# Half of the gate chunks moved into the last attention unit and the sample attention, which runs in four 32-column tiles

## The chip, the cores and the metric

The kernel runs on one core of one Trainium2 chip. The metric is the device time in microseconds of one execution. TensorE (PE in the profile) multiplies, VectorE (DVE), ScalarE (ACT) and GpSimd (POOL) work element by element, SyncE (SP) mostly issues transfers (DMA).

## What is computed

One layer of a decoder trunk, for a prompt of 1024 tokens and 8 sample sequences of 8 new tokens (T = 1088 tokens in all), D = 1024. The parts that matter here, from the reference:

```python
h = rmsnorm(x, p['pre_mix_norm'])
u = h @ p['w_in']                      # q,k,v of 3 groups, z, xbc, dt, gate_raw (2*D_MODEL columns)
# branch A: dilated attention; groups (128,1), (512,4), (2048,16), 8 heads of 64
# branch B: Mamba-2 SSD, 4 groups of 8 heads, chunked scan, gated group norm
a_proj = a_out @ p['w_attn_out']
b_proj = y @ p['w_ssd_out']
gate_a = jax.nn.sigmoid(gate_raw[..., :D_MODEL])
gate_b = jax.nn.sigmoid(gate_raw[..., D_MODEL:])
mixed = (gate_a * a_proj + gate_b * b_proj) @ p['w_out']
x = x + rmsnorm(mixed, p['post_mix_norm'])
# then a SwiGLU feed-forward with w_up and w_down

# sample attention, one sequence b with its 8 queries:
g = jnp.take(kv_all, jnp.maximum(idx, 0).reshape(-1), axis=1)     # idx = past_rows + i - j*dil
s = jnp.einsum('bshe,bskhe->bshk', q, g[:, :, :, 0]) * ATTN_SCALE
p, lse = masked_softmax_stats(s, valid)
o = jnp.einsum('bshk,bskhe->bshe', p, g[:, :, :, 1])
```

In the sample attention the softmaxes of the three groups are merged by their denominators, which is one softmax over all keys of the three groups. The 1024 past positions give 128 + 512 + 512 loaded rows per batch (of the third group 8 rows of every 16), and each batch has 24 new rows.

## The kernel before

**Layout and precision.** Activations lie transposed, channels on the partitions, tokens in three parts TH = 0:384, 384:736, 736:1088 (part c uses PSUM bank G[c]; the other five banks are A[0..4]). Each f32 operand of the big products is split into a high and a low fp32r half (hH, hL; wH, wL), and a product takes three matmuls per k-step (L2173 to L2175): hi x hi, lo x hi, hi x lo. A weight chunk is 1024 x 128 columns (512 KB): SP loads it into one of two raw buffers (wraw), GpSimd splits it (L775, L777) into one of three slots (wH, wL), TensorE uses it for the three parts. The order of chunks and of the uses of a bank is fixed by numbers: C_SSD, C_ATT, C_PROJ, C_OUT, C_FF count chunks (semaphore w_split), U_SSD, U_ATT, U_SAM, U_PROJ count uses of a bank (g_ready when filled, g_free when emptied).

**Stages, in order.** (1) norm and transposes; (2) the state-space stage, a loop over 4 groups (`group`): conv chunks, z chunks between the steps of the scan, then a state loop of four passes hp, then the output product of the group with w_ssd_out; (3) attention of the prompt, 12 units (j, gr), j = 0..3 pairs of heads, gr = 0..2 groups, each of 8 token tiles, with the q, k, v products of the next unit between the tiles (`qkv_part`); the last unit (3,2) has no next one; (4) sample attention, 8 batches b; (5) projection, gating (`mix`) and output product; (6) feed-forward.

**The state loop.** In pass hp TensorE transposes the s0 state of two heads (L2368, 8 transposes of 128x128) and VectorE and ScalarE copy the result out (s0t; ScalarE at L1173, behind its four Silus of zs, L1146). Then two parts of gate chunk hp (`tile(10 + hp, ..., only=c)`), the cm matmuls (L2379, 32 columns each, on two column tiles), the bm matmuls (L2383), and the third part of the gate chunk. So 4 gate chunks (GT = 4) belong to each group, 16 in all. ScalarE makes the sigmoid and stores it to gate_scr (`gate_part`). s0 has two buffers: a pass's state is stored, then the state of the pass after the next is loaded into the same buffer.

**Sample attention.** Per batch SP loads the keys (kraw, 9 tiles of 128 rows x 512) when those of the batch before are transposed, and the values (vraw) when the batch's value product is done. `scores(b + 1)` runs ahead of `values(b)`. TensorE transposes five key tiles per pair of heads (L2532), ScalarE copies them (L1295), and a 64-column product gives the scores of groups 0 and 1 (L2545, L2548). The keys of group 2 are multiplied and reduced on VectorE (`own_keys`) against the query rows, replicated through q_scr in DRAM; the values of group 2 are weighed and added on VectorE too (`weigh`). The scores against the new rows are computed in unit (3,2) (`new_scores`) and go through n_scr in DRAM; `new_rows` writes the new k and v rows to the outputs there, one group after the other. The softmax: masked minima on VectorE (L1876), exponential on ScalarE (L1299), scaling on VectorE (L1885). The value product is one of 64 columns with 512 moving columns per tile (L2589). Between batches 1 and 2 the prompt's attention output (atok) is transposed on four banks (L2612) and split into aH (L1323) and aL (L1940). GpSimd builds the block-diagonal queries (qblk).

**The gates.** The gates are loaded back from gate_scr and accm from ba_scr in the course of the sample attention, on SP.

## Time and profile before

| | us |
|---|---|
| median of 3 runs | 2932.91 |
| lowest, highest | 2931.29, 2938.15 |
| the profiled execution's own time | 2932.58 |
| its span | 2930.9 |

| engine | busy us | share of the span |
|---|---|---|
| PE (matmuls) | 2808.0 | 96% |
| PEld (weight loads) | 2624.9 | 90% |
| DVE | 1392.7 | 48% |
| ACT | 826.3 | 28% |
| POOL | 835.8 | 29% |

Times in the profile are microseconds from the start of the span. Matmuls overlap in the records, so the cost of one in a stream is the distance between starts, not its duration. An f32 matmul (not a transpose) stands as two records, an fp32r one as one. `x8` means eight records merged in one line. `[0.76 <-ACT ...]` is idle time of the engine before the line and what ended it. "128*32" is the stationary operand, rows x columns. The clock column is the granted TensorE clock, 1.00 for 2.4 GHz and 0.5 for 1.2 GHz, averaged over the stretch.

### The profile page before, as it was taken

The page shows a single profiled execution, that of the slowest core. Times are in us where ns is not written, and L with a number is a line of the kernel's source. Part 1 is how long each engine was busy: PE and PEld are TensorE (multiplying, and loading weights), DVE is VectorE, ACT ScalarE, POOL GpSimd, SP SyncE. Part 2 cuts the span into 40 slices and gives each one's busy share as a digit, 9 for nine tenths or more (in the row PEclk, how much of TensorE's full clock was granted, in tenths as well). Part 3 has the DMA queues.
Part 4 walks back from the last instruction along what each step waited for, and adds up shares of the span by engine and source line. Part 5 has one row for each costly group of instructions (what it writes and reads, how often), then busy time and mean ns, then how long its engine had stood idle before and what let it go on. Part 6 is the DMA issues. An engine that isn't in the chain of part 4 may idle for free.

```text
span 2930.9 us, 46443 instructions
## 1 busy us (share of the span) xinstructions
PE 2808.0 (96%) x17725; PEld 2624.9 (90%) x17725; DVE 1392.7 (48%) x2390; ACT 826.3 (28%) x1977; POOL 835.8 (29%) x554
## 2 busy tenths in 40 slices
PE   7999999999999999999999976889999999999997
PEld 5989998999999899999999963359999999999997
DVE  5485557647565762212323236677733333333334
ACT  4463155126414511333332332213410000000004
POOL 2342334324422434112121100024042323232332
PEclk9999999999999999999999988989999999999999
DMA  5545335344534532122231356973011111111111
GB/s 176 174 123 159 105 118 172 103 144 121 175 93 129 164 111 97 32 73 61 60 81 45 82 159 186 292 235 119 23 51 44 49 39 51 37 51 37 51 48 66
DMA packets 334137, 303.04 MB, mean 103 GB/s; under 512 B 26320, under 2 KB 302336, under 8 KB 332328
## 3 DMA queue, kind: packets, MB, share of 16 engines
q1 hardware_dynamic: 249464, 243.09, 27.1%
q10 hardware_dynamic: 84456, 56.93, 6.5%
q8 instruction: 152, 2.49, 0.3%
q14 instruction: 65, 0.53, 0.1%
HBM read 250.81 MB, written 102.91 MB: 121 GB/s over the span
## 4 chain that ended last, share of the span: by engine, by line
PE 89%; DVE 3%; DMA 3%; issue 2%; ACT 1%; POOL 1%; SPq 0%; ACTq 0%; DVEq 0%; POOLq 0%
PE ps L2173 24%; PE ps L2174 24%; PE ps L2175 24%; PE ps L2464 2%; PE ps L2443 2%; PE ps L2334 1%; PE ps L2330 1%; PE ps L2455 1%; PE ps L2548 1%; PE ps L2333 1%; PE ps L2532 1%; PE ps L2589 1%; DMA wraw<-in_w_out_dram 1%; DMA smqrep<-q_scr 1%; PE ps L2383 1%
## 5 line engine op out<-in xcount | busy, mean ns | idle before, releaser
L2173 PE MATMUL ps<-hH,wH 128*128 128x352 f32 (+1 forms) x2208 | 739.0, 335 | 8.7 <-issue 4.5
L2175 PE MATMUL ps<-hH,wL 128*128 128x352 f32 (+1 forms) x2208 | 722.4, 327 | 0.0
L2174 PE MATMUL ps<-hL,wH 128*128 128x352 f32 (+1 forms) x2208 | 722.2, 327 | 0.0
L775 POOL CAST wH<-wraw 128x1024 fp32r<-128x1024 f32 (+1 forms) x178 | 195.8, 1100 | 1550.3 <-PE ps L2175 1230.5
L777 POOL TENSOR_TENSOR wL<-wraw,wH 128x1024 fp32r<-128x1024 f32 (+1 forms) x178 | 443.6, 2492 | 14.3
L2173 PEld LDWEIGHTS ps<-hH,wH 128*128 128x128 f32 x2208 | 416.7, 189 | 33.8 <-issue 26.5
L2174 PEld LDWEIGHTS ps<-hL,wH 128*128 128x128 f32 x2208 | 417.2, 189 | 0.4
L2175 PEld LDWEIGHTS ps<-hH,wL 128*128 128x128 f32 x2208 | 416.1, 188 | 0.0
L2173 PE MATMUL ps<-mH,wH 128*128 128x384 f32 (+1 forms) x1128 | 371.4, 329 | 2.7 <-issue 2.7
L2174 PE MATMUL ps<-mL,wH 128*128 128x384 f32 (+1 forms) x1128 | 371.1, 329 | 1.0 <-issue 0.8
L2175 PE MATMUL ps<-mH,wL 128*128 128x384 f32 (+1 forms) x1128 | 370.1, 328 | 0.0
L1832 DVE COPY atp<-ps 128x256 f32<-128x256 f32 (+1 forms) x96 | 52.5, 547 | 363.1 <-PE ps L2455 363.1
L2173 PEld LDWEIGHTS ps<-mH,wH 128*128 128x128 f32 x1128 | 211.8, 188 | 4.3 <-issue 3.8
L2174 PEld LDWEIGHTS ps<-mL,wH 128*128 128x128 f32 x1128 | 211.6, 188 | 2.4 <-issue 1.9
L2175 PEld LDWEIGHTS ps<-mH,wL 128*128 128x128 f32 x1128 | 211.7, 188 | 0.0
L2173 PE MATMUL ps<-uH,wH 128*128 128x352 f32 (+1 forms) x528 | 174.3, 330 | 0.0
L2174 PE MATMUL ps<-uL,wH 128*128 128x352 f32 (+1 forms) x528 | 172.8, 327 | 0.0
L2175 PE MATMUL ps<-uH,wL 128*128 128x352 f32 (+1 forms) x528 | 172.8, 327 | 0.0
L2107 DVE TENSOR_TENSOR m<-m,ps 128x352 f32<-128x352 f32 (+1 forms) x240 | 123.4, 529 | 78.6 <-PE ps L2175 78.3
L1434 ACT ACTIVATE sq<-sq 128x352 f32<-128x352 f32 (+1 forms) x63 | 31.8, 507 | 416.3 <-DVE sq L2042 416.3
L949 ACT COPY qkv<-ps 128x384 f32<-128x384 f32 (+2 forms) x108 | 59.2, 548 | 311.4 <-PE ps L2175 273.0
L2088 DVE TENSOR_TENSOR sq<-sq,ps 128x352 f32<-128x352 f32 (+1 forms) x66 | 35.0, 532 | 220.0 <-PE ps L2175 220.0
(405 smaller groups left out, 4664.2 us busy)
## 6 DMA issues: line engine op xcount, KB each, us to landing
wraw<-in_w_in_dram SPq DMA_DIRECT2D x92, 512.0 KB, 3.9
wraw<-in_w_up_dram SPq DMA_DIRECT2D x44, 512.0 KB, 3.7
ssdcr<-cum_scr ACTq DMA_DIRECT2D x32, 512.0 KB, 4.5
out_dram<-in_cache_kv_w_dram SPq DMA_DIRECT2D x16, 960.0 KB, 5.5
smkraw<-in_cache_kv_w_dram SPq DMA_DIRECT2D x45, 256.0 KB, 7.1
wraw<-in_w_down_dram SPq DMA_DIRECT2D x22, 512.0 KB, 3.6
smkraw<-in_cache_kv_w_dram SPq DMA_DIRECT2D x9, 1024.0 KB, 6.4
smvraw<-in_cache_kv_w_dram SPq DMA_DIRECT2D x35, 256.0 KB
```

What stands on the lines that cost most here:

```text
L775: pool.tensor_copy(hi, a).then_inc(w_hi, 1)
L777: pool.tensor_tensor(lo, a, hi.bitcast(F32), ALU.subtract).then_inc(w_split, 1)
L949: ins = act.copy(dst, src)
L1434: act.activation(cols(sq[i], c), cols(sq[i], c), ACT.Silu).then_inc(gate_silu, 1)
L1832: dve.tensor_copy(pt[(i - 1) % 2][:, :, :].rearrange("p a b -> p (a b)")[:, 0:w], A[3][:, 0:w]).then_inc(pt_out, 1)
L2088: dve.tensor_tensor(cols(sq[i], c), cols(sq[i], c), gff(c, 2 * i + 2), ALU.mult).then_inc(g_free[c], 1)
L2107: dve.tensor_tensor(cols(m2[:, m, :], c), cols(m2[:, m, :], c), gff(c, m + 1), ALU.add).then_inc(g_free[c], 1)
L2173: pe.matmul(dst, hi, cols(mH[:, k, :], c), start=k == 0, stop=False)
L2174: pe.matmul(dst, hi, cols(mL[:, k, :], c), start=False, stop=False)
L2175: last = pe.matmul(dst, lo, cols(mH[:, k, :], c), start=False, stop=k == kt - 1)
L2443: mm = pe.matmul(score_half(gr, t, s), tokens(qT, gr, t)[rows], keys(kT, gr, t)[rows], start=True, stop=True)
L2464: mm = pe.matmul(A[4][:, 64 * s:64 * s + 64], pt[i % 2][:, s * len(bl) + b, :], vtok[gr][:, t, 64 * s:64 * s + 64], start=b == 0, stop=b = ...
```

## The change

Two gate chunks instead of four stay in each state-space group (GT = 2); a pass of the state loop now has three halves of a part (`gate_half`) at three places. Eight chunks move: three into unit (3,2), as its products (`unit_gate`), five into the sample attention, as 119 + 1 single k-steps at six places of each batch (`fill`, FILL). Their raw values are stored by ScalarE (`moved_store`), and the sigmoid is made after they are loaded back (`sigmoids`, in the projection stage, for rows 4 to 7 of each gate). The w_ssd_out chunks are six instead of four.

In the sample attention all three groups go through TensorE: 36 key transposes per batch on three banks, copied in turn by ScalarE and VectorE into buffers for the whole batch; the scores and the values as sets of four 32-column tiles (`quarter`), one per pair of heads, so that 128 partitions hold the scores; the new rows' scores are computed in each batch; the probabilities are not scaled, the output is. `own_keys`, `weigh`, q_scr, n_scr and newS go. The new k and v rows are transposed within units (3,1) and (3,2) (`sets`). The batches no longer overlap, and the loops over them are unrolled. The transposes of atok move into the last batch, on two banks. The buffers lie elsewhere (kraw and vraw over the qkv region), and so the loads of gates and accm come later on SP.

The diff, cut to what the prediction speaks of:

```diff
-GT = 4
+GT = 2
...
-U_SAM = U_ATT + NJ * NG * 3
+NGC = 2 * KD - GT * SG
+U_SAM = U_ATT + NJ * NG * 3 + 3
...
+WSSD = ((0, 2), (2, 2), (4, 1), (5, 1), (6, 1), (7, 1))
...
+        FILL = {(b, s): n for b in range(DB - 1) for s, n in enumerate((2, 2, 9, 1, 1, 2))}
+        FILL[DB - 1, 0] = 1
+        assert sum(FILL.values()) == (NGC - 3) * 3 * KD
...
-            firsts += [GATE0 + k * D + g * 2 * P + m * P for m in range(2) for k in range(2)]
+            firsts += [GATE0 + k * D + g * P for k in range(GT)]
             return [(win[:, :, ds(f, P)], KD, P) for f in firsts] + [
-                (wssd_rows(g)[:, :, m * 2 * P:(m + 1) * 2 * P], XT, 2 * P) for m in range(KD // 2)]
+                (wssd_rows(g)[:, :, m * P:(m + n) * P], XT, n * P) for m, n in WSSD]
...
+                    sp.wait_ge(s_ready, tiles - NT)
+                    sp.wait_ge(vt_ready, tiles - NT)
+                    sp.wait_ge(kvn_out[0], 16 * 4)
+                    load_k(0)
+                    for y in range(3, 7):
+                        load_gate_chunk(y)
+                    send_unit(NJ - 1, 2)
+                    merge_store(2)
+                    sp.wait_ge(s_ready, tiles)
+                    sp.wait_ge(vt_ready, tiles)
+                    sp.wait_ge(kvn_out[1], 16 * 2)
+                    load_v(0)
+                    merge_load(NJ - 1)
+                    load_new(0)
+                    for b in range(DB - 1):
+                        sp.wait_ge(k_fill, 12 * b + 9)
+                        load_k(b + 1)
+                        if b == 0:
+                            sp.wait_ge(pv_ready, tiles)
+                            sp.wait_ge(a_out, 16 * (NJ - 1))
+                            for j in range(NJ - 1):
+                                sp.dma_start(atok[:, :, j * P:(j + 1) * P], a_scr[j]).then_inc(at_in, 16)
+                            load_gate_chunk(7)
+                        if b == 5:
+                            load_proj(0)
+                            sp.wait_ge(mg, MG * NJ)
+                            for c in range(3):
+                                sp.wait_ge(gate_out[c], 16 * (GT * SG + 6) + 1)
+                            load_gates(0, SG, KD - 1)
+                        if b == 6:
+                            load_proj(1)
                         sp.wait_ge(spv_ready, b + 1)
                         load_v(b + 1)
                         load_new(b + 1)
...
...
-                    sp.dma_start(accm[:, 0:4, :], ba_scr[:, 0:4, :]).then_inc(ba_in[0], 16)
+                        sp.wait_ge(gate_out[c], 32 * KD + 1)
+                    sp.wait_ge(mt_ready, NT)
+                    sp.wait_ge(g_free[2], U_SAM + DB)
+                    sp.wait_ge(sm_dve, 4 * DB - 2)
+                    load_gates(0, 0, SG)
+                    load_gates(0, KD - 1, KD)
+                    sp.dma_start(accm[:, :, TH[0][1]:T], ba_scr[:, :, TH[0][1]:T]).then_inc(ba_in[1], 16)
+                    load_proj(3)
+                    sp.wait_ge(spv_ready, DB)
+                    sp.wait_ge(gates_in, 16 * 6)
                     load_gates(1)
-                    sp.wait_ge(aL_ready, NT + 1)
-                    sp.dma_start(accm[:, 4:8, :], ba_scr[:, 4:8, :]).then_inc(ba_in[1], 16)
+                    sp.wait_ge(gates_in, 16 * 8)
+                    sp.wait_ge(mix_step, 3 * KD)
...
-                        pool.wait_ge(ysq_ready, g * XT + k - 12)
-                        if k > 14:
-                            pool.wait_ge(ysum_done, g * (XT - 1) + k - 14)
+                    for m in {SG_W + 1: (1,), SG_W + 2: (2, 3)}.get(k, ()):
+                        pool.wait_ge(ysq_ready, g * XT + m + 1)
+                        if m > 1:
+                            pool.wait_ge(ysum_done, g * (XT - 1) + m - 1)
...
                     y_parts(hp)
-                    gate_part(hp, 1)
+                    if hp == 0:
+                        gate_part(0, 0)
+                    if hp == 2:
+                        gate_part(1, 0)
                     act.wait_ge(s0_new, g * 12 + 3 * hp + 3)
...
-                        act.wait_ge(ssm_out, g * 64 + 16 * hp + 16)
-                        load_s0(hp + 2)
+                    if hp == 1:
+                        gate_part(0, 2)
                     if hp == 3:
                         act.wait_ge(st_out, g * 16 + 16)
                         roots(XT, g * SSD_USES + (U_SSD + 11 + GT), (0, 1))
-                    gate_part(hp, 2)
...
+            def sigmoids(c):
+                act.wait_ge(gates_in, 16 * (6, 8, 10)[c])
+                for k in range(2):
+                    act.activation(gates[c][k][:, SG:KD, :], gates[c][k][:, SG:KD, :], ACT.Sigmoid).then_inc(gate_sig, 1)
...
                     if hp == 0:
                         dve.wait_ge(yev_done, g * NCH + NT)
                     dve.wait_ge(zs_silu, g * XT + hp + 1)
                     dve.tensor_tensor(xs[:, hp, 0:SEQ], xs[:, hp, 0:SEQ], zs[:, hp, 0:SEQ], ALU.mult).then_inc(gate_done, 1)
+                    for b in range(DB):
+                        ins = dve.tensor_scalar(s[:, b, :], s[:, b, :], ecd[:, hp, b:b + 1], None, ALU.mult)
+                    ins.then_inc(s0_new, 1)
                     dve.wait_ge(s0_new, g * 12 + 3 * hp + 1)
                     dve.wait_ge(s0_up, g * 4 + hp + 1)
...
+                def gate_half(q):
+                    c, t = q // 2 % 3, q // 6
+                    if q % 2 == 0:
+                        if c == 0:
+                            pe.wait_ge(w_split, g * SSD_CH + (C_SSD + 10 + t + 2))
+                        bank(c, use(11 + t))
+                    for k in range(4 * (q % 2), 4 * (q % 2) + 4):
+                        mm = gate_step(gap(c), (C_SSD + 10 + t) % SPL, k, c)
+                    if q % 2:
+                        mm.then_inc(g_ready[c], 1)
                 pe.wait_ge(st_ev, g + 1)
...
-                    for c in range(2):
-                        tile(10 + hp, hH, hL, KD, use(11 + hp), only=c)
+                    gate_half(3 * hp)
...
+                    gate_half(3 * hp + 1)
                     if hp == 3:
                         pe.wait_ge(ysum_done, g * (XT - 1) + XT - 1)
                         y_sums(0)
                         y_sums(1)
-                    tile(10 + hp, hH, hL, KD, use(11 + hp), only=2)
+                    gate_half(3 * hp + 2)
...
                                 mm.then_inc(s_ready, 1)
-                    if nxt is not None and i <= NT:
-                        qkv_part(*nxt, i)
+                    if i <= NT:
+                        if nxt is not None:
+                            qkv_part(*nxt, i)
+                        else:
+                            unit_gate(i)
...
+            def fill(b, s):
+                a = steps_before(b, s)
+                for q in range(a, a + FILL.get((b, s), 0)):
+                    p, k = q // KD, q % KD
+                    x, c, bk = p // 3, p % 3, p % 2
+                    if k == 0:
+                        if c == 0:
+                            pe.wait_ge(w_split, C_GATE + 3 + x + 2)
+                        pe.wait_ge(g_free[bk], U_SAM + p // 2)
+                    mm = gate_step(gap2(bk, c), (C_GATE + 3 + x) % SPL, k, c)
...
+            def ring(b, f):
+                n = f - 3 if f >= 3 else f + 9
+                e = b if f >= 3 else b - 1
+                if e >= 0:
+                    pe.wait_ge((kt_act, kt_dve)[n % 2], 6 * e + n // 2 + 1)
+                return A[f % 3]
+            def keys_of(b, f):
+                bank = ring(b, f)
+                for x in range(4):
+                    t, j = (0, x) if f == 0 else (1 + (f - 1) % 2 * 4 + x, (f - 1) // 2)
+                    mm = pe.transpose(bank[:, x * P:(x + 1) * P], kraw[:, t, j * P:(j + 1) * P], ident[:, :])
+                mm.then_inc(k_fill, 1)
+            def quarter(a, j):
...
+            def scores(b):
+                pe.wait_ge(kt_act, 6 * b + 5)
+                pe.wait_ge(kt_dve, 6 * b + 4)
+                pe.wait_ge(qb_ready, b + 1)
+                if b:
+                    pe.wait_ge(aS_out, b)
+                for j in range(NJ):
+                    pe.matmul(quarter(A[3], j)[:, 0:P], heads_q(0, j), kt_g0[:, j, :], start=True, stop=True)
+                for gr in range(NG):
+                    for j in range(NJ):
+                        o = P + DS * gr
+                        mm = pe.matmul(quarter(A[3], j)[:, o:o + DS], heads_q(gr, j), qkvs[:, 1, gr, j, b * DS:b * DS + DS],
+                                       start=True, stop=True)
+                mm.then_inc(sc_ready, 1)
+                if b:
+                    pe.wait_ge(sm_dve, 4 * b - 2)
+                for j in range(NJ):
+                    mm = pe.matmul(quarter(A[4], j), heads_q(1, j), kt_g1[j][:, :], start=True, stop=True)
+                mm.then_inc(sc_ready, 1)
+                bank(2, U_SAM + b + 1)
+                for j in range(NJ):
+                    mm = pe.matmul(quarter(G[2], j), heads_q(2, j), kt_g2[j][:, :], start=True, stop=True)
+                mm.then_inc(g_ready[2], 1)
...
+            def values(b):
+                pe.wait_ge(v_in, 144 * b + 144)
+                pe.wait_ge(kt_dve, 6 * b + 5)
+                for t in range(9):
+                    if t == 3:
+                        pe.wait_ge(kt_act, 6 * b + 6)
+                    if t == 7:
+                        pe.wait_ge(kt_dve, 6 * b + 6)
+                    for j in range(NJ):
+                        pe.matmul(quarter(A[3], j)[:, 0:P], pts[:, t * NS + 16 * j:t * NS + 16 * j + 32], vraw[:, t, j * P:(j + 1) * P],
+                                  start=t == 0, stop=False)
+                for j in range(NJ):
+                    mm = pe.matmul(quarter(A[3], j)[:, 0:P], pts[0:24, 9 * NS + 16 * j:9 * NS + 16 * j + 32],
+                                   vnew[b % 2][:, j * P:(j + 1) * P], start=False, stop=True)
+                mm.then_inc(spv_ready, 1)
...
+            for b in range(DB):
+                pe.wait_ge(k_in, 96 * b + 96)
+                for f in range(5):
+                    keys_of(b, f)
+                fill(b, 0)
+                for f in range(5, 9):
+                    keys_of(b, f)
+                fill(b, 1)
+                scores(b)
+                fill(b, 2)
+                if b == DB - 1:
+                    pe.wait_ge(mg, MG * NJ)
+                    pe.wait_ge(at_in, 16 * (NJ - 1))
+                    pe.wait_ge(g_free[0], U_SAM + DB)
+                    pe.wait_ge(g_free[1], U_SAM + DB - 1)
+                    for i in range(NT):
+                        if i >= 2:
+                            pe.wait_ge(aL_ready, i - 1)
+                        for j in range(NJ):
+                            mm = pe.transpose(G[i % 2][:, j * P:(j + 1) * P], atok[:, i, j * P:(j + 1) * P], ident[:, :])
+                        mm.then_inc(mt_ready, 1)
+                pe.wait_ge(sm_exp, b + 1)
+                for f in range(9, 12):
+                    probs(b, f)
+                fill(b, 3)
+                values(b)
+                fill(b, 4)
                 pe.wait_ge(sO_out, b + 1)
...
+                pe.transpose(A[3][:, P:2 * P], sO[:, :], ident[:, :]).then_inc(sOt_ready, 1)
+                fill(b, 5)
+            pe.sem_inc(g_ready[1], 1)
```

## Rows read from the trace of the kernel before

**Rows 1.** page of before: span and clock in 40 slices
```profile
span 2930.9 us, 46443 instructions
...
PEclk9999999999999999999999988989999999999999
```

**Rows 2.** stretch, its us, busy time of PE, PEld, DVE, ACT, POOL busy, clock, DMA
```profile
73.00:1110.00 1037.00, 1030.36 (x6943) 973.92 (x6944) 644.58 (x833) 400.63 (x804) 376.41 (x200) 1.00 0.43 134
1711.00:1742.00 31.00, 20.98 (x179) 16.73 (x179) 9.44 (x50) 13.65 (x58) 1.49 (x8) 0.80 0.85 264
1742.00:1945.00 203.00, 147.87 (x578) 68.10 (x578) 135.86 (x213) 47.06 (x117) 32.15 (x64) 0.86 0.82 243
```

**Rows 3.** timeline, two product parts: start us, us, engine, line, operation
```profile
1641.20 0.34 PE L2174 MATMUL ps<-hL,wH 128*128 128x384 f32 x1
...
1645.02 0.34 PE L2175 MATMUL ps<-hH,wL 128*128 128x384 f32 x1
...
1646.86 0.32 PE L2174 MATMUL ps<-hL,wH 128*128 128x352 f32 x1
...
1650.37 0.32 PE L2175 MATMUL ps<-hH,wL 128*128 128x352 f32 x1
```

**Rows 4.** timeline of PE and ACT in the state loops of groups 0 and 1
```profile
213.41 1.09 PE L2368 MATMUL ps<-ident,ssds 128*128 128x128 f32 x8
...
218.51 0.56 ACT L1173 COPY ssds0t<-ps 128x512 f32<-128x512 f32 x1
...
222.48 1.07 PE L2379 MATMUL ps<-ssds0t,cm 128*32 128x128 f32 x16
223.48 1.13 PE L2383 MATMUL ps<-bm,ssdxe 64*128 64x512 f32 x4
...
479.50 1.09 PE L2368 MATMUL ps<-ident,ssds 128*128 128x128 f32 x8
...
484.60 0.56 ACT L1173 COPY ssds0t<-ps 128x512 f32<-128x512 f32 x1
```

**Rows 5.** DMA issues of ACT in 212 to 275: count, KB each, median us to landing
```profile
out_dram<-ssds ACTq DMA_DIRECT2D x4, 512.0 KB, 3.3
ssds<-in_state_ssm_dram ACTq DMA_DIRECT2D x2, 512.0 KB, 4.4
```

**Rows 6.** timeline of PE at the ends of units (2,1) and (2,2)
```profile
1559.55 1.08 PE L2464 MATMUL ps<-atv,atp 128*128 128x64 f32 x8 [0.47 <-DVE ato L1835]
...
1606.39 0.63 PE L2464 MATMUL ps<-atv,atp 128*128 128x64 f32 x4 [0.47 <-DVE ato L1835]
```

**Rows 7.** timeline of PE in one batch of sample attention
```profile
1860.56 1.31 PE L2532 MATMUL ps<-ident,smkraw 128*128 128x128 f32 x10 [0.20 <-issue]
...
1873.15 4.48 PE L2589 MATMUL ps<-smvraw,smpt 128*64 128x512 f32 x10 [0.97 <-DVE smpt L1889]
...
1880.39 0.43 PE L2597 MATMUL ps<-ident,smkvn 64*128 64x64 f32 x4 [0.76 <-ACT smkvn L1308]
1881.00 1.20 PE L2532 MATMUL ps<-ident,smkraw 128*128 128x128 f32 x9 [0.18 <-issue]
```

**Rows 8.** timeline of ACT and DVE: a cast, a subtraction and an exponential
```profile
1821.18 0.59 ACT L1323 CAST aH<-ps 128x512 fp32r<-128x512 f32 x1 [0.27 <-PE ps L2612]
...
1821.80 0.69 DVE L1940 TENSOR_TENSOR aL<-ps,aH 128x512 fp32r<-128x512 f32 x1 [0.16 <-ACT aH L1323]
...
1880.87 1.28 ACT L1299 ACTIVATE sms<-sms,small 64x1176 f32<-64x1176 f32 x1 [0.62 <-DVE small L1881]
```

**Rows 9.** DMA issues in 1742 to 1945, the key loads of eight batches
```profile
smkraw<-in_cache_kv_w_dram SPq DMA_DIRECT2D x40, 256.0 KB, 7.1
smkraw<-in_cache_kv_w_dram SPq DMA_DIRECT2D x8, 1024.0 KB, 6.7
```

**Rows 10.** busy time per stretch, columns as in rows 2
```profile
1830.00:1910.00 80.00, 67.00 (x271) 29.01 (x269) 54.45 (x88) 20.28 (x52) 6.77 (x33) 0.94 0.97 292
...
1880.00:1890.00 10.00, 8.54 (x39) 4.81 (x40) 6.89 (x10) 4.40 (x11) 0.00 (x0) 0.83 0.96 276
```

719 lines of the change are left out of this document (271 added, 448 removed).

## The prediction

> **What bounds the kernel now.** I read the page first. TensorE is the bound nearly everywhere: it sits in the chain that ended last with 89% and its clock is full but for the slices around 1,700 to 1,950 us [rows 1]. Then a table by stage [rows 2]: in the state-space stage (73 to 1110) TensorE is busy 1030 of 1037 us at clock 1.00, so there a matmul taken out is time taken out. In 1711 to 1742 (last attention unit) it is busy 21 of 31 us at 0.80, and in 1742 to 1945 (sample attention) 148 of 203 us at 0.86. Those two stages, 234 us, wait for other engines, transfers and a slow clock; nothing there is filled with independent work. So the question is what 234 us of waiting stage becomes when gate products are put into it, against what the full stage gives back.
>
> **Price of a gate chunk.** A chunk is 8 k-steps x 3 token parts x 3 matmuls. In a full stretch 22 starts of 384 columns take 3.82 us and 22 of 352 columns 3.51 us [rows 3], so 0.1736 and 0.1596 us each: a chunk is 24 x (0.1736 + 2 x 0.1596) = 11.8 us. One step (three matmuls) is 0.49 us. The same 16 chunks are computed; 8 move.
>
> **State-space stage: what comes back.** Two chunks fewer in each of 4 groups: 8 x 11.8 = 94.6 us. Not all of it: the chunks were the cover of the state loop (four passes). In pass 0 TensorE ends the state transposes at 214.50, then needs ScalarE's copy of s0t, which stands behind four Silus and ends at 219.07; the other groups look alike (479.50 and 484.60 + 0.56) [rows 4]. Before, 8 us of gate product lay in between; after it, half a part, 4 steps of 0.52 = 2.1 us. That leaves 219.07 - 214.50 - 2.1 = 2.5 us, x4 groups = 10 us. A pass shrinks from 1.1 + 11.8 + 1.0 + 1.1 = 15 us (transposes, chunk, cm and bm matmuls [rows 3, 4]) to 1.1 + 3 x 2.0 + 2.1 = 9.2 us. Late next is the s0 ring: s0 store to landing 3.3 us, load 4.4 us [rows 5]; update ready about 7.7 us into a pass, then ScalarE's issue, store and load: 7.7 + 0.7 + 3.3 + 0.7 + 4.4 = 16.8 us against two passes of 18.4. It fits by 1.6 us. GpSimd's last ysum add ends about when TensorE asks for it. I take 2 us in all for both. The eight tensor_scalars that replace one broadcast multiply on VectorE lie under the pass. Two extra, half-size weight chunks on SP and GpSimd replace two gate chunks: same count of loads and splits, nothing. Gain: 94.6 - 10 - 2 = 82.6 us.
>
> **Last two attention units.** Unit (3,2) before had no products and took 31 us. With three gate chunks it is a unit like any other of its group: unit (2,2) runs from 1559.55 to 1606.39, 46.8 us [rows 6]. The 24 added k/v-row transposes at 0.107 us are 2.6 us in both units; the q_scr and n_scr round trips, and new_rows with its three rounds of store and wait, go. So sample attention starts at 1711 + 46.8 + 2.6 = 1760.4 on the old scale instead of 1742.
>
> **Sample attention, one batch.** Own TensorE work after: 36 key transposes; 10 back to back start within 1.31 - 0.24 = 1.07 us [rows 7], so 3.85. Scores: one set of four 32-column tiles with 128 columns, 12 tiny ones, two sets with 512. Five f32 matmuls of 512 columns (x10) take 4.48 us with the tail, so one matmul 0.86 alone [rows 7], one of 128 columns 0.214. Do four column tiles run at once? The trace shows two: 8 matmuls of 128*32 (each stands twice in the records, hence x16) on two column tiles take 1.0 us to the next instruction [rows 4], where 8 one after another would be 8 x 0.214 = 1.71. Four at once isn't in the trace. Bounds: a set costs one matmul (0.86 and 0.21) or four (3.4 and 0.86). I take one, since the second tile cost nothing. Scores then: 0.21 + 0.3 + 2 x 0.86 = 2.2; probabilities 10 x 0.107 = 1.1; values 10 sets x 0.214 = 2.1; output transpose 0.1. Sum 9.3 us. Fill: 17 steps = 8.4 us. Hand-overs: a batch before had 14 us of work (20 + 4 transposes, 4 x 1.07 of scores, 7 x 0.86 of values, 14 small ones) in a period of 1881.00 - 1860.56 = 20.4 us [rows 7], so 6 us of waits and slow clock; the fill covers most of them. The softmax: VectorE passes of 0.69 for 512 columns and ScalarE's exponential 1.28 [rows 8] make a chain of 0.3 + 0.7 + 0.2 + 1.5 + waits, about 3.7 us after the last scores, under 9 steps = 4.4 us. The 0.5 us steps after probabilities and values do not cover a PSUM copy and two waits (0.76 us idle at the output copy before [rows 7]). I take 2.6 us. Period 9.3 + 8.4 + 2.6 = 20.3 us.
>
> **The transfers.** Keys are 5 x 256 + 1024 KB = 2.36 MB a batch, values as many [rows 9]; 80 us before moved data at 292 GB/s with the engines' share at 0.97 [rows 10]. At 292: 16.2 us for keys and values, 2.6 us for gate weights and stores: 18.8 against 20.3, so TensorE still sets the period, narrowly. At the start it doesn't. On SP, load_v(0), merge_load(3) and load_new(0) stand behind send_unit(3,2), which waits for the end of the unit: 1.6 MB of unit output, 0.5 MB of merge store, 2.4 MB of values, 1.6 MB of mb, then vnew: 6.1 MB = 21 us plus 3. values(0) can start at 25 us instead of 15.5; TensorE idles 9.5 us and goes on at half clock (2 us). Keys of batch 1 queue behind: batch 1 starts at 33. atok (1.6 MB), a weight chunk and values 1 come before keys 2: batch 2 starts at 55.3. Then five periods: batch 7 at 156.8. It has no fill: keys and scores 9, then eight atok tiles on two banks instead of four (0.43 + 0.58 + 0.69 and waits = 2.1 per two, 8.4 [rows 8]), behind the exponential at 12; probabilities, values, output and the last aL: 26 us. Sum 182.8. So projection starts at 1760.4 + 182.8 = 1943 instead of 1944.5: about 62 us of added products for nothing.
>
> **Projection.** Gates and accm now load late, behind mt_ready; the six sigmoids (1536 columns each) go to ScalarE, idle there. VectorE's first mix waits for about 1.5 us beyond TensorE's start, six banks run ahead. I take 2 us. The rest is unchanged.
>
> **Sum.** Profiled execution 2932.58 (span 2930.9 and 1.7 around it), within 0.4 us of the median. 2932.6 - 82.6 - 1.3 + 2 = 2850.7; I add 1.3 for a clock that falls once more in batches 0 and 1: 2852.
>
> **Where the skill speaks.** In 1880 to 1890, with key transposes and scores, the granted clock was 0.83, one stretch at 1.2 GHz [rows 10]. The Trainium skill, "TensorE: Matmul & The Clock Gate", Part 4, says that transposes don't count as busy for the clock gate as matmuls do. By that rule, 36 transposes a batch instead of 20 keep the fall. The trace agrees in part: the fall is there, though other work lay around it.
> The same page, Part 3 ("Measured speedup vs the span model"), gives 2.38x for three column tiles and not 3x. By that, an estimate, sets would cost 1.26 times as much, 1 us a batch, and the sum would be 2860.
>
> **The rivals.**
> A, forecast: 2852, own range 2836 to 2868. Chance 0.52.
> B, the clock falls once per batch after, too (0.17 x 10 = 1.7 us lost in rows 10): 8 x 1.7 = 14, 2866. For it: transposes are the same work; against: products between them. 0.15.
> C, transfers set the period: at the stage's mean of 243 GB/s [rows 2] a batch needs 22.5 us: 7 x 2.2 + 5 at the start = 20, 2872. For it: the share stood at 0.97 for 80 us [rows 10]. 0.13.
> D, two column tiles at once, not four: 2 x 0.86 + 0.2 + 2.1 = 4 us a batch, 32 us: 2884. 0.07.
> E, the change doesn't give back what it moves: the s0 ring or ScalarE holds each pass at 12 us instead of 9.2: 16 x 2.8 = 45 us, 2897. Against: VectorE and ScalarE are at 645 and 401 of 1037 us [rows 2]. 0.07.
> F, slower: column tiles run one after another. Place: the score and value sets; price 2 x 2.6 + 0.6 + 10 x 0.64 = 12.2 us a batch, 97 us: 2949. It decides from 10 us a batch. Against: two tiles did overlap. 0.04.
> 0.02 is left for faster than A: a first batch without the wait, 2830.
>
> **How the numbers follow.** The likeliest is A, 2852. Range 2836 to 2886 holds A, B, C and D: 0.85 or so. Within 0.2% (5.9 us, about what a measurement of this kernel tells from no change) of before needs a mix of E and D: 0.02. Slower: F and mishaps of E with D, 0.04. Faster 0.94.
>
> **What would show it.** State-space groups 20 us shorter each, with 2.5 us idle ahead of the first cm matmuls; unit (3,2) near 48 us; ten value sets in 2.1 us (D 4.3, F 8.5); waits of 10 us for values 0 and 5 for keys 1; a period of 20.3 from batch 2; granted clock near 1.00 there (B: 0.9). Wrong if a pass waits for s0_in (E), or if TensorE waits for keys in every batch (C).

## The result and the profile after

The changed kernel takes 2888.8 us (median of four, 2884.2 to 2890.0) beside 2932.3 us before: ratio 0.984, interval 0.983 to 0.986. Forecast was 2852, range 2836 to 2886: the direction is right, the gain is 44 us instead of 81, and the time lies 3 us above the range.

The page of after, and its table by stage with the stretches of [rows 2] (stretch, its us, busy time of PE, PEld, DVE, ACT, POOL, clock, DMA share, GB/s):

```profile
span 2888.2 us, 47476 instructions
...
PEclk9999999999999999999999998999999999999998
```
```profile
73.00:1110.00 1037.00, 1001.53 (x6689) 936.79 (x6690) 651.55 (x964) 398.64 (x810) 375.97 (x225) 0.99 0.42 130
1711.00:1742.00 31.00, 17.30 (x191) 13.62 (x189) 3.81 (x16) 3.97 (x8) 0.52 (x2) 0.78 1.02 266
1742.00:1945.00 203.00, 181.93 (x1827) 159.41 (x1828) 95.57 (x207) 64.24 (x112) 30.92 (x28) 0.95 0.88 260
```

Against [rows 2], sample attention is filled (182 of 203 us busy instead of 148), but the state-space stage, which had 7 idle us in 1037, now has 35, though the windows no longer cut at the same work. A fixed window misleads once work has moved, so I cut at the same instructions in both traces. The marks of after are these rows of TensorE's timeline (start us, us, engine, line, operation): first state transposes of groups 0 and 1 (L2359), the end of state loop 0 (L2319), first attention unit (L2433), sample attention (L2515), projection (L2145); the last stage ends with TensorE's last matmul:

```profile
215.02 1.09 PE L2359 MATMUL ps<-ident,ssds 128*128 128x128 f32 x8
...
259.51 0.46 PE L2319 MATMUL ps<-ident,ssdytok 64*128 64x64 f32 x4
...
467.15 1.09 PE L2359 MATMUL ps<-ident,ssds 128*128 128x128 f32 x8
...
1095.41 0.30 PE L2433 MATMUL ps<-ident,qkv 128*128 128x128 f32 x1 [0.81 <-ACT qkvs L965]
...
1706.28 0.98 PE L2515 MATMUL ps<-ident,kraw 128*128 128x128 f32 x7 [0.81 <-DVE ato L1852]
...
1899.22 0.44 PE L2145 MATMUL ps<-aH,wH 128*128 128x384 f32 x1 [1.38 <-DVE aL L1924]
```

The same marks of before are 213.41 and 479.50 [rows 4], 274.64, 1148.65, 1741.84 and 1944.51. From them, in us (minus is time saved; the forecast's column is its own working):

| stretch | before | after | change | forecast |
|---|---|---|---|---|
| start to state loop 0 | 213.4 | 215.0 | +1.6 | 0 |
| the four state loops | 244.9 | 177.3 | -67.6 | -82.6 |
| what lies between and behind the loops | 690.3 | 703.1 | +12.8 | 0 |
| attention units | 593.2 | 610.9 | +17.7 | +18.4 |
| sample attention | 202.7 | 192.9 | -9.7 | -19.9 |
| projection to the last matmul | 976.7 | 979.4 | +2.7 | +2, and 1.3 for the clock |

So 38 us are missing: 15 in the loops, 13 between them, 10 in sample attention, 2 ahead of it all (the start of loop 0 ranges over 212 to 217 in the traces of changed kernels, so that is no effect), less 1.3 that the attention units and the last stage gained on the forecast. The experiments go through the three large ones.

### The profile page after: what moved, and what is told of

Read it like the earlier page. It is cut to its first block, busy times and chain, and to the rows that moved or that the text cites. A ratio compares the mean times of both kernels' runs of the same rounds, so it can differ in the third digit from the quotient of the medians.

```text
span 2888.2 us, 47476 instructions
## 1 busy us (share of the span) xinstructions
PE 2766.8 (96%) x18529; PEld 2633.0 (91%) x18529; DVE 1331.5 (46%) x2462; ACT 832.1 (29%) x1952; POOL 822.3 (28%) x505
## 4 chain that ended last, share of the span: by engine, by line
PE 85%; DVE 3%; DMA 3%; ACT 2%; issue 2%; SPq 2%; POOL 1%; ACTq 1%; DVEq 0%; POOLq 0%
PE ps L2145 23%; PE ps L2146 22%; PE ps L2147 22%; PE ps L2471 2%; PE ps L2447 2%; DMA kraw<-in_cache_kv_w_dram 1%; PE ps L2313 1%; PE ps L2309 1%; PE ps L2462 1%; PE ps L2153 1%; PE ps L2515 1%; PE ps L2154 1%; PE ps L2155 1%; PE ps L2312 1%; DMA wraw<-in_w_out_dram 1%
## 5 line engine op out<-in xcount | busy, mean ns | idle before, releaser
L2145 PE MATMUL ps<-hH,wH 128*128 128x384 f32 (+1 forms) x1896 | 636.1, 336 | 16.2 <-issue 5.2
L791 POOL CAST wH<-wraw 128x1024 fp32r<-128x1024 f32 (+2 forms) x186 | 195.1, 1049 | 1521.7 <-PE ps L2147 1164.1
L2146 PE MATMUL ps<-hL,wH 128*128 128x384 f32 (+1 forms) x1896 | 622.1, 328 | 0.0
L2147 PE MATMUL ps<-hH,wL 128*128 128x384 f32 (+1 forms) x1896 | 622.1, 328 | 0.0
L793 POOL TENSOR_TENSOR wL<-wraw,wH 128x1024 fp32r<-128x1024 f32 (+2 forms) x186 | 447.8, 2407 | 14.9
L2145 PEld LDWEIGHTS ps<-hH,wH 128*128 128x128 f32 x1896 | 359.3, 189 | 32.9 <-issue 23.3
L2145 PE MATMUL ps<-mH,wH 128*128 128x384 f32 (+1 forms) x1128 | 371.3, 329 | 3.6 <-issue 3.6
L2146 PEld LDWEIGHTS ps<-hL,wH 128*128 128x128 f32 x1896 | 359.5, 190 | 0.0
L2147 PEld LDWEIGHTS ps<-hH,wL 128*128 128x128 f32 x1896 | 358.8, 189 | 0.0
L2145 PEld LDWEIGHTS ps<-mH,wH 128*128 128x128 f32 x1128 | 211.8, 188 | 5.2 <-issue 4.8
L2145 PE MATMUL ps<-uH,wH 128*128 128x352 f32 (+1 forms) x528 | 174.7, 331 | 0.0
```

The costliest lines, as they stand in the source:

```text
L791: pool.tensor_copy(hi, a).then_inc(w_hi, 1)
L793: pool.tensor_tensor(lo, a, hi.bitcast(F32), ALU.subtract).then_inc(w_split, 1)
L2145: pe.matmul(dst, hi, cols(mH[:, k, :], c), start=k == 0, stop=False)
L2146: pe.matmul(dst, hi, cols(mL[:, k, :], c), start=False, stop=False)
L2147: last = pe.matmul(dst, lo, cols(mH[:, k, :], c), start=False, stop=k == kt - 1)
```

## The experiments

### The same kernel again

No edit.

> The changed kernel once more, unchanged, to see which of its idle times come back in a second execution. Theory: the idle times that an engine of this core causes come back to within 0.3 us (2.8 us ahead of the first cm matmuls of each of the four state loops, 1.1 us for GpSimd's sum of squares in each loop, 12.4 us for the values of batch 0). Those at the back edge of the loop over groups (3.8 and 5.2 us at 320 and 572) vary, since the record names nothing that they wait for: anything from 0 to 6 us each. Rival: all of them come back, because they are caused by the supply of weights. Time 2884 to 2890 us.

2885.8 us. The idle times that an engine causes came back: 2.8, 2.9, 2.8, 2.6 us ahead of the first cm matmuls, 1.1 us for GpSimd's sum (1.0 in the last loop); values 0 were waited for 11.4 us, off by 1.0 and more than the 0.3 I allowed. At the ends of groups 0 and 1 the idle times were 3.5 and 4.2 instead of 3.8 and 5.2: present, but variable. Sample attention took 191.4 us instead of 192.9.

### The end of a group

```
-            with pe.Fori(0, SG - 1) as g:
-                group(g, g + 1)
-            group(SG - 1, None)
+            for g in range(SG):
+                group(g, g + 1 if g < SG - 1 else None)
```

> The changed kernel, but TensorE's program has the four state-space groups written out instead of a loop of three and one; all other engines are unchanged. Theory: the two idle times of 3.8 and 5.2 us at the ends of groups 0 and 1, and the half-clock stretches of 6.8 us that follow them, are the jump back at the loop's end; they go: 9 + 2 x 2 to 3 = 13 to 15 us less, 2874 to 2876. Rival: they are the wait for the weights split by GpSimd (one of them ends with that split), and stay: 2889. A third outcome is that straight code has to be loaded too and costs some us elsewhere.

2866.9 us (2861.9 to 2868.8), ratio 0.977 (0.976 to 0.979): 19 to 22 us less than the two results of the changed kernel, more than expected. After, TensorE stops at 320.6 and 572.6 and goes on here (idle time and its supposed cause in brackets), and the windows behind the first stop give half clock (0.50) at once:

```profile
324.38 0.68 PE L2145 MATMUL ps<-hH,wH 128*128 128x384 f32 x1 [3.78 <-POOL wL L793]
...
577.76 0.68 PE L2145 MATMUL ps<-hH,wH 128*128 128x384 f32 x1 [5.18 <-issue]
```
```profile
320.60:324.40 3.80, 0.02 (x2) 0.02 (x1) 3.18 (x5) 0.62 (x3) 3.38 (x2) 0.89 0.07 27
324.40:328.00 3.60, 3.60 (x11) 3.60 (x12) 2.33 (x3) 1.21 (x1) 0.00 (x0) 0.50 0.56 118
```

The first row names GpSimd's weight split, the second nothing. The unrolled kernel shows which is right. Its timeline of GpSimd and of TensorE at the same place:

```profile
316.43 1.04 POOL L791 CAST wH<-wraw 128x1024 fp32r<-128x1024 f32 x1 [8.17 <-PE ps L2147]
317.55 2.40 POOL L793 TENSOR_TENSOR wL<-wraw,wH 128x1024 fp32r<-128x1024 f32 x1
```
```profile
315.94 0.32 PE L2147 MATMUL ps<-hH,wL 128*128 128x352 f32 x1
316.09 0.34 PE L2145 MATMUL ps<-hH,wH 128*128 128x384 f32 x1
```

The split ends at 319.95, as late against TensorE as before, and TensorE starts the next tile at 316.09 without a pause. So the split was never waited for, and the stop is the jump back at the loop's end. The rival falls. The branch itself is in the traces. These rows give, for the branch at the end of TensorE's loop, shortest, median and longest duration in ns, and when the first and the last one start: of after, then of before (L2410 there). The third row is the instruction transfer in 321.7 to 322.8 of after (packets, MB, share):

```profile
L2403 PEldq COMPARE_BRANCH  x3: 83/6417/7813, 317.7 to 823.1; - x3
```
```profile
L2410 PEldq COMPARE_BRANCH  x3: 83/3523/6156, 332.8 to 860.8; - x3
```
```profile
q8 instruction: 1, 0.02, 5.3%
```

The third branch, which leaves the loop, takes 0.08 us; the two that jump back take 6.4 and 7.8 us in after. The first starts at 317.7, 2.9 us before TensorE's last matmul ends at 320.60, as the queue had run ahead of the array; what is left of it is the stop. All eight traces of changed kernels with the loop have both stops (2.1 to 5.2 us, branches of 4.8 to 7.8 us), the four with the groups written out have none. In 17 of the 18 stops (the two of before among them) TensorE goes on 2.6 to 3.0 us after a 16 KB instruction transfer has started (queue q8, which elsewhere has one every 14 to 25 us; that it is TensorE's is inferred from this pace). The Trainium skill, "Runtime: NRT & Kernel Launch", section "Instruction fetch mechanics", says that a taken branch to code that isn't at hand forces a fetch of it before execution goes on. This case agrees: the branch ends and TensorE goes on only after such a transfer, and the stop goes when the branch goes. The other engines, whose loops stayed, could not be told apart here.

### Does the jump cost the kernel before as much?

The same edit in the kernel before.

> The kernel before, with TensorE's program for the four state-space groups written out instead of a loop of three and one. Theory: the jump back costs the kernel before less than the changed one (idle 3.6 and 0.9 us in its trace, against 3.8 and 5.2, and a shorter half-clock stretch), so this gains 6 to 9 us, 2924 to 2927, against 15 to 20 us that the same edit gave the changed kernel. Then 8 to 12 us of the expected gain went into that jump. Rival: it gains as much here (15 to 20 us, 2913 to 2918): then the jump is a cost of both kernels and explains nothing of the miss.

2928.2 us, ratio 0.9986 (0.9976 to 0.9996): 4 us, 1 to 7 by the interval. That is less than the 6 to 9 expected, though the interval reaches into them, and far from the rival's 15. The stops of before are these:

```profile
339.30 0.43 PE L2173 MATMUL ps<-hH,wH 128*128 128x384 f32 x1 [3.58 <-issue]
...
602.70 0.44 PE L2173 MATMUL ps<-hH,wH 128*128 128x384 f32 x1 [0.89 <-issue]
```

From the end of one state loop to the start of the next, in us:

| kernel | group 0 to 1 | 1 to 2 | 2 to 3 |
|---|---|---|---|
| before | 204.9 | 200.7 | 199.2 |
| before, written out | 199.2 | 199.2 | 199.2 |
| after | 207.6 | 209.2 | 200.7 |
| after, again | 206.2 | 206.1 | 199.6 |
| after, written out | 203.2 | 199.6 | 199.4 |

The third column has no jump and nearly no loss. Both kernels do the same products here. Stops and half clock together, the jump costs 7 us in the trace of before (against 199.2), and 18 and 13 in the two of after (against 199.4; 10 to 17 in the other six traces of changed kernels that have the loop); by medians 4 against 19 to 22. Not all of those 19 to 22 us lie at the jump: in the traces the stretches between the loops gave 15 and 10 us (687.8 instead of 703.1 and 697.4), the state loops 4, because pass 0 came without half clock in three groups, and sample attention 3 to 4, which no run explains. Of the missing 38 us the stretches between the loops hold 13; the jump is 11 of them (18 against 7), the rest is 1.5 us in the third column, without a jump, which also varies (199.2 to 200.7). Why the jump costs the changed kernel more is known in part. Its two branches last 14.2 and 13.0 us together in after and its repetition and 10.3 to 13.0 in the six others, those of before 9.7 in its one trace; the instruction transfer that ended the stop had started 0.7 us after TensorE stopped and 1.9 us before it in before, 1.2 and 2.2 us after it in after. Why it starts later is open. The transfer itself took 0.9 to 1.3 us in all but one case (2.1 us, with 4.1 us to the end of the stop), so contention with other transfers lengthened it at most there (27 GB/s were moved in the first stop, row above).

### The stall of pass 0

```
                 for m in range(XT):
                     act.activation(zs[:, m, :], zs[:, m, :], ACT.Silu).then_inc(zs_silu, 1)
+                    if m == 0:
+                        act.wait_ge(s0_tr, g * 4 + 1)
+                        act.copy(s0t[:, 4:8, :]..., A[4][:, :]).then_inc(s0t_act, 1)
```

> The changed kernel, but ScalarE copies the first s0t of a group behind the first of its four Silus instead of behind the fourth. Theory: the 2.8 us of idle TensorE and the half-clock stretch that follows it (the cm and bm matmuls of that pass take 1.9 us more than in pass 1) go in all four groups, pass 0 falls from 13.8 to about 9.2 us: 4 x 4.6 = 18 us less, 2871. Rival 1: the clock falls anyway, only the idle time goes: 11 us, 2878. Rival 2: the Silus, now later by one copy, hold the gating multiplications and through them the later passes: the loop stays at 44.4 us and the time at 2889.

2877.8 us, ratio 0.980 (0.978 to 0.982): 8 to 11 us. That is rival 1's number, but not its mechanism: the half clock did go with the stall. The stall itself had been as forecast (2.8 us, 2.5 in the prediction), but the matmuls behind it ran at half speed. Of after, pass 0 and pass 1:

```profile
221.01 1.81 PE L2369 MATMUL ps<-ssds0t,cm 128*32 128x128 f32 x16 [2.79 <-ACT ssds0t L1189]
222.76 2.02 PE L2373 MATMUL ps<-bm,ssdxe 64*128 64x512 f32 x4
...
231.74 1.07 PE L2369 MATMUL ps<-ssds0t,cm 128*32 128x128 f32 x16
232.74 1.13 PE L2373 MATMUL ps<-bm,ssdxe 64*128 64x512 f32 x4
```

With the early copy pass 0 fell from 13.8 to 9.3 us in every group, and pass 1 rose from 8.9 to 11.2 to 11.8 and pass 2 from 10.1 to 11.0 to 11.4. So the four loops took 176.2 us, only 1 to 2 less than in after and its repetition; most of the 8 to 11 us lies outside the loops, where the edit changes nothing, and is not explained. TensorE and ScalarE of that kernel, group 0 (first its store of the updated states, then its load for pass 2):

```profile
227.57 0.38 ACTq L1207 DMA_DIRECT2D out_dram<-ssds  x1
...
234.20 0.40 ACTq L1107 DMA_DIRECT2D ssds<-in_state_ssm_dram  x1
```
```profile
238.50 1.97 PE L2363 MATMUL ps<-ident,ssds 128*128 128x128 f32 x8 [2.77 <-DMA ssds<-in_state_ssm_dram]
```

The loop began at 217.40: states of pass 2 are there 21.1 us later, where two passes are 18.4. That is the buffer ring that the prediction put at 16.8 us.

### Without the ring

The early copy, and the loads of passes 2 and 3 left out (cut; the waits for the stores stand behind, ahead of the next use of the buffer):

```
                     if 1 <= hp < 3:
-                        act.wait_ge(ssm_out, g * 64 + 16 * hp)
-                        load_s0(hp + 1)
+                        pass
```

> As the kernel with s0t copied early, but the states of passes 2 and 3 of each group are not loaded (left out: the load of half of the states; the old contents are used again), so that no pass waits for a buffer to be stored and loaded. Theory: with the stall of pass 0 gone, pass 1 lengthened from 8.9 to 11.2 to 11.8 us because pass 2's states had not landed; without the ring pass 1 is 8.9 again, the loop 40.5 to 41.5 instead of 43.3 to 45.5, and the time 10 to 14 us under that of s0t_first: 2864 to 2868. Rival: pass 1 stays near 11.5, since VectorE or ScalarE holds it: 2878.

2858.5 us (2856.4 to 2860.7), ratio 0.975 (0.974 to 0.977), 19 us under the kernel with the early copy: more than the 10 to 14 expected; the loops gave 16.5 of them. Each of the four loops took 39.9 us, passes 9.3, 8.9, 10.1 and 11.7. So the ring did hold pass 1; the rival falls. What is still above the forecast's 9.2 lies in passes 2 and 3.

### The eight small multiplications

```
-                    for b in range(DB):
-                        ins = dve.tensor_scalar(s[:, b, :], s[:, b, :], ecd[:, hp, b:b + 1], None, ALU.mult)
-                    ins.then_inc(s0_new, 1)
```
(and the one broadcast multiplication of before, ahead of the gating product)

> The changed kernel with one part of the change undone: the states are decayed by one broadcast multiplication on VectorE ahead of the gating product, as before, instead of by eight small ones behind it. Theory (my prediction costed this part at nothing): the time stays within 3 us, 2884 to 2890, loops 44.3. Rival: pass 2, in which the eight small ones took 3.9 us beside GpSimd's work instead of 1.65, is 0.7 us shorter, and pass 0, where the broadcast one runs beside GpSimd's split, longer or not: loops 43 to 43.6, 3 to 5 us less.

2880.7 us (2878.3 to 2883.7), ratio 0.982 (0.981 to 0.984): 5 to 8 us less. Pass 2 took 9.2 instead of 10.1 us in all groups, 3.5 us in sum; one pass 0 came without half clock, 1.6 us shorter, and the rest is within what executions of the changed kernel differ by. VectorE in pass 2 of after, and of this kernel:

```profile
239.39 3.23 DVE L1701 TENSOR_TENSOR xs<-xs,zs 128x1024 f32<-128x1024 f32 x1
242.54 3.90 DVE L1703 TENSOR_SCALAR ssds<-ssds,small 128x128 f32<-128x128 f32 x8
```
```profile
239.49 3.23 DVE L1698 TENSOR_TENSOR ssds<-ssds,small 128x1024 f32<-128x1024 f32 x1
242.65 1.21 DVE L1703 TENSOR_TENSOR xs<-xs,zs 128x1024 f32<-128x1024 f32 x1
```

And GpSimd in pass 2 of after:

```profile
239.16 2.38 POOL L793 TENSOR_TENSOR wL<-wraw,wH 128x1024 fp32r<-128x1024 f32 x1
243.96 2.41 POOL L852 TENSOR_TENSOR ysum<-ysum,ysq 128x1024 f32<-128x1024 f32 x1 [2.43 <-ACT ysq L1174]
```

VectorE's first operation takes 3.2 us in both kernels (the gating product takes 1.2 in pass 1 of after) and lies on the weight split. The eight small ones take 3.9 us here and 1.65 in pass 1; the sum of squares lies on them. The Trainium skill, "SBUF — State Buffer", section "Who interferes with whom", calls this a shared port pair that one of the two engines holds for a whole instruction. The rows agree: the gating product is lengthened by 2.0 us where the split lies on it for 2.2, the eight small ones by 2.3 where the sum of squares takes 2.4. Placed behind the gating product, the multiplications met a second GpSimd operation.

### The waits for the first values and keys

```
                     load_v(0)
-                    merge_load(NJ - 1)
-                    load_new(0)
+                    sp.wait_ge(unit_out[2], 16 * 6 * NJ + 1)
+                    load_new(0)
+                    merge_load(NJ - 1)
```

> The changed kernel, but the three small loads of the new value rows of batch 0 are issued ahead of the 1.6 MB of the last merge load, behind the same wait. Theory: the 12.4 us wait for the values of batch 0 is mostly the 8.7 us that the queue's engine spends on issuing the merge load ahead of them; it falls to about 4 us, and as the transfers behind it stay in order, batch 1 starts only a few us earlier: 3 to 8 us less, 2881 to 2886. Rival: the transfers are the bound of the first three batches (the engines' share is 0.9 or more throughout); the wait moves to the keys of batches 1 and 2 and the time stays within 2 us, 2889.

2884.6 us, ratio 0.983 (0.981 to 0.985; one of its four times, 6887 us, is left out of the ratio). In after, SyncE's queue spends 8.7 us on the merge load ahead of three small loads, and the values wait for those:

```profile
1720.93 8.72 SPq L576 DMA_DIRECT2D mgb<-o_scr  x3
1729.69 1.61 SPq L592 DMA_DIRECT2D vnew<-out_dram  x3
```
```profile
1735.03 4.07 PE L2570 MATMUL ps<-vraw,pts 128*32 128x128 f32 x72 [12.42 <-DMA vnew<-out_dram]
```

With the order turned round the wait fell to 7.1 us, and the keys took over (waits of TensorE in the first three batches: for whom, us in total, times, longest):

```profile
PE ps L2516 <- DMA kraw<-in_cache_kv_w_dram: 12.0, 2, 6.7
PE ps L2571 <- DMA vnew<-out_dram: 7.1, 1, 7.1
```

Batches 0 to 2 together took 87.2 us, where after had 86.1 and its repetition 84.9. The time lies within the theory's 2881 to 2886, but by the trace of these batches the rival holds: the order doesn't matter.

### Fewer bytes

```
+                n = 1 if isinstance(j, int) and j == NJ - 1 else NT
-                    sp.dma_start(mb[:, :, gr, :], o_scr[j, gr]...)
+                    sp.dma_start(mb[:, 0:n, gr, :], o_scr[j, gr]...[:, 0:n, :])
```

> The changed kernel, but the last merge load brings one eighth of its rows (left out: 1.4 of the 1.6 MB of unit output that the last merge reads again). Theory: from the end of the last unit until batch 3 the transfers are the bound, so 1.4 MB less at 250 to 290 GB/s make batch 3 start 4 to 6 us earlier, in the waits for values 0 and keys 1: 2881 to 2885. Rival: the waits are of an order, not of an amount: batch 3 starts as late as before, 2888.

2875.9 us, ratio 0.982 (0.980 to 0.984), but over 2868.1 to 2887.5. By the trace, batches 0 to 2 took 77.3 us: 7.6 to 8.8 less for 1.4 MB, more than the 4 to 6 of the theory. In the other traces that do not change these batches they took 82.3 to 87.2 us, so the gain is 5 us at the least. The amount of data matters, so the transfers are the bound there; why the gain is larger than 1.4 MB at 250 to 290 GB/s is open.

### The price of the fill

```
-                    mm = gate_step(gap2(bk, c), (C_GATE + 3 + x) % SPL, k, c)
                     if k == KD - 1:
+                        mm = pe.matmul(gap2(bk, c), wH[...][:, k * P:(k + 1) * P], cols(hH[:, k, :], c),
+                                       start=True, stop=True)
```

> The changed kernel with the fill left out (of each of the 15 parts of 24 matmuls that were put between the steps of sample attention only one matmul is computed: 345 matmuls, 57 us, are missing, and with them five chunks of the gates). Theory: in batches 3 to 5 TensorE sets the period with the fill (19.0 us), so without it the period is the larger of the batch's own chain and its transfers: 14 to 17 us; with 3 us less in each of 7 batches but more waits for transfers in the first three, 15 to 25 us less: 2864 to 2874. Rival 1: the transfers already set the period: it stays at 18.5 to 19 and the time within 5 us of the changed kernel. Rival 2: all 57 us of the fill are on the path: 2832.

2871.8 us (2870.2 to 2874.6), ratio 0.980 (0.978 to 0.981). Its first attention unit started 9 us earlier than that of after, which is not the edit's doing, so it is luck that the whole time lies within the theory's 2864 to 2874. The stage is what to read: sample attention took 184.9 us instead of 192.9 and 191.4. The 57 us of products cost 7 to 8, or 2 to 9 by the range that the stage had in the traces where nothing in it was edited (187.3 to 193.5). Batches 3 to 6 took 19.4, 16.3, 20.4 and 21.1 us, mean 19.3, with TensorE busy two thirds of the time, at a clock of 0.89, and the transfers at a share of 1.00 (columns as above):

```profile
1777.00:1854.00 77.00, 50.91 (x709) 38.51 (x709) 24.18 (x70) 23.11 (x44) 8.88 (x12) 0.89 1.00 300
```

Beside it the first and two later batches of after:

```profile
1706.00:1743.00 37.00, 22.02 (x226) 18.05 (x226) 5.98 (x20) 5.86 (x11) 2.76 (x3) 0.82 0.97 246
...
1792.00:1811.00 19.00, 19.00 (x228) 16.26 (x227) 5.92 (x17) 5.86 (x11) 3.96 (x4) 1.00 0.89 262
1811.00:1830.00 19.00, 19.00 (x228) 16.33 (x227) 5.88 (x18) 5.97 (x11) 0.52 (x2) 1.00 0.91 271
```

In the later batches TensorE never stops with the fill (19.00 of 19.00), and the transfers need as long without it. The two are balanced, so rival 1's period (18.5 to 19) holds within a microsecond and my 14 to 17 falls.

### Together

The groups written out, the early copy, and in pass 0 the store of the states ahead of the gate part:

> The changed kernel with three edits together: TensorE's four groups written out, s0t copied behind the first Silu, and in pass 0 the store of the updated states issued ahead of the gate part instead of behind it. Theory: the jump is worth 15 to 20 us as before; the early copy alone is worth little because the states of pass 2 come back 21 us after the start of pass 0 at the earliest (loop 43.3 to 45.5); with the store 1.2 us earlier passes 0 and 1 together take 20 us and the loop 42 to 43 us instead of 44.3: 2 us x 4 on top, 2856 to 2862, the fastest of all. Rival 1: ring and jump are worth what they were alone and add up fully (19 + 8 to 11): 2857 or less with loops of 43.5. Rival 2: the early copy is worth nothing once the jump is gone (pass 0 had 12.0 us there already): 2866.

2868.4 us, ratio 0.978 (0.977 to 0.980), no faster than the groups written out alone: rival 2. Loops of 42.6 to 44.4 us, as there (42.8 to 44.2). Pass 0 had no half clock in three groups there and took 12.0; here it takes 9.3, but in group 0 TensorE waits 1.5 us for the states at the end of pass 1 and another 2.0 for VectorE at the end of pass 2 (11.5).

Then the groups written out with the broadcast multiplication, and all four edits:

> The changed kernel with TensorE's groups written out and the states decayed by the one broadcast multiplication. Theory: the two gains add, since they lie in different places (the end of a group, pass 2 of its state loop): 19 to 22 us and 3.5 to 8 us off 2886 to 2889: 2858 to 2864, loops 42 to 43 us with pass 2 at 9.2. Rival: what pass 2 gives back is lost again at the next wait (GpSimd's sum of squares in pass 3): loops 43.3 as in the kernel with only the groups written out, 2867.

> The combination of three edits (groups written out, s0t copied early, store of the states ahead of the gate part), and the broadcast multiplication too. Theory: the early copy was worth nothing in the combination because pass 2 waited another 2.0 us for VectorE's update of pass 1's states, which stood behind the eight small multiplications and GpSimd; with the broadcast one this wait goes and pass 0 keeps its 9.3 us: loops of 40 to 41.5 us instead of 42.6 to 44.4, 2856 to 2861. Rival: the states of pass 2 come back no earlier than 20 us after the loop's start whatever VectorE does: passes 0 and 1 stay at 19.9, loops at 41.5 to 42.5, no faster than the kernel without the early copy.

2863.6 us (2854.0 to 2867.7), ratio 0.976 (0.974 to 0.978), and 2857.6 us (2852.2 to 2865.6), ratio 0.975 (0.973 to 0.976). The second beats both kernels: 28 to 31 us under the changed one, and 6 under the first (within the spread of the two, but the loops of its trace are 4.5 us shorter). The first gained 3 us on the groups written out alone, within the spread, so whether the gains add is not settled; pass 2 took 9.2 us in all four groups, but pass 0 again 13.6 to 14.9 in three. In the second, pass 2 fell to 9.3 in three groups, and pass 3 rose by 1.2 through GpSimd's sum; loops 42.1 to 42.8 us, not 40 to 41.5. Passes 0 and 1 stayed at 19.8 to 20.4: there the rival named the ring rightly.

State loops side by side (group 0, us):

| kernel | pass 0 | 1 | 2 | 3 | sum |
|---|---|---|---|---|---|
| before | 15.0 | 15.0 | 15.0 | 16.3 | 61.2 |
| after | 13.8 | 8.9 | 10.1 | 11.7 | 44.5 |
| early copy | 9.3 | 11.8 | 11.0 | 11.6 | 43.8 |
| early copy, no ring | 9.3 | 8.9 | 10.1 | 11.7 | 39.9 |
| broadcast multiplication | 13.8 | 8.9 | 9.2 | 11.7 | 43.6 |
| all edits | 9.3 | 10.5 | 9.3 | 12.9 | 42.1 |

## Why the prediction was off

**Price of a chunk.** Right: pass 1, where nothing waits, is 6.1 us shorter for half a chunk less (5.9 by the price).

**State loops.** Mechanism right, sizes off. The 2.5 us stall was 2.8. The step that failed is its price: I counted the idle time and no slower clock behind it, which adds 1.8 us to pass 0 of each group. (The whole loop loses less by it: where pass 0 came without it and took 12.0 to 12.2 us, pass 2 took 10.4 to 11.1 instead of 10.1, waiting for VectorE, and the loop 42.8 to 43.5 us instead of 44.1 or more.) "2 us in all for both" (ring and GpSimd) is the other one: pass 2 is 1.1 us above 9.0, pass 3 1.3 above its share (16.3 less 5.9), 2.4 us in each of four groups. By group: 0.3 for the stall, 1.8 for the clock, 2.4 here; times four and less the 2 allowed that is 16 us, for 15 measured. The eight multiplications were "under the pass"; they were not, in pass 2. The ring, 16.8 us by my sum, is 21.1: update ready at 8.5 instead of 7.7, store issued 1.6 later instead of 0.7, 6.6 us until the load could be issued instead of 3.3 and 0.7 (the store took 6.5 us to land), and 4.3 for the load. It is hidden in after only because pass 0 stalls. So rival E was right in kind, not in size (11.1 us a pass instead of 12).

**Rest of a group.** The prediction has no term for it beyond "nothing" for two more weight chunks. That nothing was right: without a jump the stretch is 199.2 us before and 199.4 after. The failed step is a term that was left out, the jump at the end of a group, and it could have been seen: groups 0 and 1 of before lie 266.1 us apart [rows 4], but in its trace groups 2 and 3 only 260.4, with the same work. 13 us, of which the jump is 11.

**Attention units.** 17.7 us for forecast 18.4.

**Column tiles.** Right: nine value sets start within 2.10 us (an f32 set of four is eight records, so x72), and the tenth, with the new rows, makes 2.45 us to the next instruction, for forecast 2.1. D (4.3) and F (8.5) fall.

```profile
1807.26 2.17 PE L2570 MATMUL ps<-vraw,pts 128*32 128x128 f32 x72
1809.36 0.42 PE L2573 MATMUL ps<-vnew,pts 24*32 24x128 f32 x8
1809.71 0.43 PE L2153 MATMUL ps<-hH,wH 128*128 128x352 f32 x1
```

With the prediction's 0.214 us for one, the 36 of the nine sets one after another would be 7.7 us (an estimate): 3.7 times as fast. The Trainium skill, "TensorE: Matmul & The Clock Gate", section "Measured speedup vs the span model", gives 2.38x for three; here four tiles reach more for each tile than that, and the sum of 2860 worked out from it falls.

**Batches.** Forecast starts of batches 1 and 2 were +33 and +55.3, measured 37.2 and 63.6. The failed step is the backlog of transfers. For batch 0 it is the rate: I took 292 GB/s, and the first 37 us ran at 246 with a share of 0.97. By that rate the 6.1 MB take 25 us plus 3 instead of 21 plus 3, and values 0 started at 28.8 instead of 25. In batch 1 (26.5 us instead of 22.3) the rate was 282 GB/s, and the amount was too small: 7.5 MB moved, where 22.3 us at 292 are 6.5. Batch 2 took 22.5 us instead of 20.3 for another reason: VectorE worked on the last merge of the prompt's attention (6.5 us, to 1786.06) ahead of its copies of the probabilities, and TensorE waited 2.0 us for them and went on at half clock:

```profile
1779.55 6.51 DVE L1788 TENSOR_TENSOR mgb<-mgb,mgarg 128x1024 f32<-128x1024 f32 x3
...
1786.60 2.90 PE L2570 MATMUL ps<-vraw,pts 128*32 128x128 f32 x72 [1.98 <-DVE pts L1906]
```

From batch 3 the period is 19.0, 19.1, 20.0 and 23.2 us for 20.3 forecast, the last with 4.1 us of waiting for keys 7. The transfers' 18.8 us was good; TensorE's own 20.3 was 1.3 too high. Rival C was right that transfers set the pace, but only in batches 0 and 1 (share 0.98 and 1.04; 0.74 in batch 2). Batch 7 took 25.5 us for 26.

**Clock.** 1.00 in batches 3 to 5, with 36 transposes each, so B falls there; it was 0.82, 0.87 and 0.92 in batches 0 to 2 and 0.88 in batch 7, which have waits of TensorE of 2 to 12 us. The Trainium skill, "TensorE: Matmul & The Clock Gate", Part 4, says that transposes don't count as busy for the clock gate as matmuls do; the trace does not contradict it, since products lay between them, and with the fill left out the clock of batches 3 to 6 was 0.89 (row above), with more waits as well.

**Projection and rest.** 2.7 us for 3.3.
